# Order of the attention steps in a turn, and of the first slabs of the output projections, in a two-block transformer kernel

## The reference

```python
hn = rmsnorm(x, norm_mix)                      # block 1
x = x + softmax_attention(hn @ w_qkv) @ w_o    # 16 heads of 64, causal
x = x + (silu(conv(gate)) * conv(up)) @ w_down
x = rmsnorm(x, norm_final)
x = x + 0.5 * (1 + ga1) * swiglu(modulate(rmsnorm(x), sh1, sc1))   # block 2
h = modulate(rmsnorm(x), sh2, sc2)
proj = h @ w_in           # q, k, v of 8 stick-breaking and 8 forgetting heads, and f
x = x + (1 + ga2) * concat(stick_breaking(...), forgetting(...)) @ w_o
x = x + 0.5 * (1 + ga3) * swiglu(modulate(rmsnorm(x), sh3, sc3))
```

## Time and profile before

| | |
|---|---|
| median of 3 runs | 852.37 us (851.05 to 853.18) |
| the profiled execution | 851.69 us, of it 849.4 us from the first to the last instruction (span) |
| TensorE matmul, weight load | 810.8 us, 788.7 us busy (95%, 93%) |
| VectorE, ScalarE | 644.5 us, 489.4 us busy (76%, 58%) |
| DMA | 179.44 MB, 211 GB/s in the mean |
| mean granted TensorE clock | 0.995 |

### The profile page before, as it was taken

The page is one execution under the profiler, slowest core; times in us unless marked ns, Lnnn a source line. Parts: engine busy times, 40 slices in busy tenths (PEclk is TensorE's granted clock), DMA queues, the critical chain, the costliest instruction groups (busy, mean ns, idle before and its releaser), DMA issues. The chain is left out here.

```text
span 849.4 us, 16846 instructions
## 1 busy us (share of the span) xinstructions
PE 810.8 (95%) x6824; PEld 788.7 (93%) x6824; DVE 644.5 (76%) x1332; ACT 489.4 (58%) x1015; POOL 21.1 (2%) x53
## 2 busy tenths in 40 slices
PE   5799998999999999999999999899989999999998
PEld 5798887999999999999999999778888999999998
DVE  5687767988898886999888776867657797665551
ACT  6745455767766666755554645655645675555440
POOL 1000000000000000000000002500000000000000
PEclk9999999999999999999999999999999999999999
DMA  9766563865565987599989885545224578665540
GB/s 296 266 220 204 159 202 132 279 195 194 197 220 177 318 279 244 153 317 351 315 290 309 279 262 150 149 130 182 87 76 140 183 255 282 210 197 186 186 150 26
DMA packets 151069, 179.44 MB, mean 211 GB/s; under 512 B 5712, under 2 KB 141136, under 8 KB 150992
## 3 DMA queue, kind: packets, MB, share of 16 engines
q1 hardware_dynamic: 149536, 177.65, 63.7%
q10 hardware_dynamic: 432, 0.68, 0.2%
q0 software_dynamic: 1024, 0.03, 0.1%
HBM read 177.27 MB, written 1.05 MB: 210 GB/s over the span
## 5 line engine op out<-in xcount | busy, mean ns | idle before, releaser
L907 DVE TENSOR_TENSOR wlo<-raw,whi 128x512 fp32r<-128x512 f32 x528 | 343.1, 684 | 71.4 <-ACT whi L669 70.8
L1279 PE MATMUL bank<-A,whi 128*128 128x256 f32 x1280 | 366.5, 286 | 14.6 <-DVE wlo L907 9.0
L669 ACT ACTIVATE whi<-raw 128x512 fp32r<-128x512 f32 x528 | 308.3, 622 | 111.3 <-PE bank L1281 101.5
L1280 PE MATMUL bank<-A,whi 128*128 128x256 f32 x1280 | 358.2, 280 | 0.0
L1281 PE MATMUL bank<-A,wlo 128*128 128x256 f32 x1280 | 358.1, 280 | 0.0
L1279 PEld LDWEIGHTS bank<-A,whi 128*128 128x128 f32 x1280 | 244.6, 191 | 18.5 <-DVE wlo L907 9.6
L1280 PEld LDWEIGHTS bank<-A,whi 128*128 128x128 f32 x1280 | 242.7, 190 | 1.0 <-issue 1.0
L1281 PEld LDWEIGHTS bank<-A,wlo 128*128 128x128 f32 x1280 | 242.3, 189 | 0.0
L1279 PE MATMUL bank<-Hhi,whi 128*128 128x256 f32 x528 | 147.7, 280 | 0.0
L1280 PE MATMUL bank<-Hlo,whi 128*128 128x256 f32 x528 | 147.5, 279 | 0.0
L1281 PE MATMUL bank<-Hhi,wlo 128*128 128x256 f32 x528 | 147.5, 279 | 0.0
(11 more groups left out here) (149 smaller groups left out, 787.8 us busy)
## 6 DMA issues: line engine op xcount, KB each, us to landing
mring<-in_w_mod SPq DMA_DIRECT2D x72, 512.0 KB, 6.2
raw<-in_ffn_w_up SPq DMA_DIRECT2D x22, 1024.0 KB, 5.1
raw<-in_w_gate SPq DMA_DIRECT2D x22, 1024.0 KB, 6.0
raw<-in_w_up SPq DMA_DIRECT2D x22, 1024.0 KB, 5.9
raw<-in_w_down SPq DMA_DIRECT2D x16, 1024.0 KB, 5.4
raw<-in_w_in SPq DMA_DIRECT2D x12, 1024.0 KB, 5.6
raw<-in_moba_w_qkv SPq DMA_DIRECT2D x11, 1024.0 KB, 5.5
raw<-in_ffn_w_down SPq DMA_DIRECT2D x8, 1024.0 KB, 6.0
```

The lines of the kernel that those rows point to most:

```text
L669: act.activation(whi[:, i % SPL, k0:k1, 0:width], raw[:, i % RAW, k0:k1, 0:width], ACT.Copy).then_inc(s_whi, 1)
L907: dve.tensor_tensor(lo, raw[:, i % RAW, k0:k1, 0:width], hi.bitcast(F32), ALU.subtract).then_inc(s_wlo, 1)
L1279: pe.matmul(o, hi, xh, start=kg == 0 and not (j and halved(g)), stop=False)
L1280: pe.matmul(o, hi, xl, start=False, stop=False)
```

## The change

Three parts. (1) In `attend()` the pairs in flight advance first and the new pair enters after them. (2) Pair B enters at A's age 3 in the last blocks too, and in qkv3 the pairs whose slabs lie at columns from 2048 on (the forgetting ones) are unlocked after 3 turns instead of 2. (3) With `O_SPLIT = 3`, o1 and o3 begin with k-tiles 0 to 5 of columns 0, 256 and 512, then k-tiles 6 and 7 of the three, then columns 768 whole; the third group accumulates in bank 4 and waits for the exponentials of head 12 (28) instead of an eviction. One slab more in each phase moves the slab numbers in the conditions by one and by two; the number of `mod` steps in each phase stays.

```diff
--- before.py
+++ after.py
@@ -28,6 +28,7 @@
 VC = {name: 8 * i for i, name in enumerate(VEC)}
 LAST_AGE = 6
 LAG = 1
+O_SPLIT = 3
 RAW = 3
 SPL = 3
 MR = 3
@@ -62,10 +63,10 @@
     def o_slabs(w):
         cut = []
         for lo_k, hi_k in ((0, 6), (6, 8)):
-            for c0 in (0, C):
+            for c0 in range(0, O_SPLIT * C, C):
                 src = w[lo_k * P:hi_k * P, c0:c0 + C].rearrange("(k p) c -> p k c", p=P)
                 cut.append(("o", c0, lo_k, hi_k - lo_k, hi_k == KD, C, src))
-        return cut + slabs_of("o", w, KD, range(0, D, C))[2:]
+        return cut + slabs_of("o", w, KD, range(0, D, C))[O_SPLIT:]
 
     up, down, w_in = a["ffn_w_up"][0], a["ffn_w_down"][0], a["w_in_2"][0]
     allc = range(0, D, C)
@@ -86,9 +87,9 @@
 
 
 MOD_STEPS = {
-    "qkv1": lambda i: int(i > 2) + int(i in (4, 7, 10)), "o1": lambda i: int(i < 17), "up1": lambda i: int(i in (30, 34)),
-    "down1": lambda i: int(i < 51), "up2": lambda i: int(i >= 56) * (1 + int(i % 4 == 0)), "down2": lambda i: int(i < 84),
-    "qkv3": lambda i: int(i in (90, 92, 94, 96)), "o3": lambda i: 0, "up4": lambda i: int(i > 108) * int(i % 2 == 0), "down4": lambda i: 0}
+    "qkv1": lambda i: int(i > 2) + int(i in (4, 7, 10)), "o1": lambda i: int(i < 18), "up1": lambda i: int(i in (31, 35)),
+    "down1": lambda i: int(i < 52), "up2": lambda i: int(i >= 57) * (1 + int(i % 4 == 1)), "down2": lambda i: int(i < 85),
+    "qkv3": lambda i: int(i in (91, 93, 95, 97)), "o3": lambda i: 0, "up4": lambda i: int(i > 110) * int(i % 2 == 0), "down4": lambda i: 0}
 QKV3_TILE = {0: 0, 512: 8, 1024: 16, 1536: 4, 2048: 12, 2560: 20}
 
 
@@ -234,13 +235,12 @@
                 pair[1] += 1
             if flight and flight[0][1] == LAST_AGE:
                 advance(*flight.pop(0))
-            old = list(flight)
-            if waiting and (not flight or flight[-1][1] > (1 if len(self.heads) % 16 > 12 else 2)):
+            for pair in flight:
+                advance(*pair)
+            if waiting and (not flight or flight[-1][1] > 2):
                 enter()
-            for pair in old:
-                advance(*pair)
             turns[0] += 1
-            pend(not any(pair[1] in (3, 4) for pair in old))
+            pend(not any(pair[1] in (3, 4) for pair in flight))
 
         group, o_group, prev = 0, 0, None
         begun, ready = 0, []
@@ -332,7 +332,7 @@
                         st.put("latelo", ph, n - 1)
                     if n == KD - 1:
                         st.put("latelo", ph, n)
-                if scaling and kt % 4 == 3 and i > 56:
+                if scaling and kt % 4 == 3 and i > 57:
                     st.put("xscale", scaling.pop(0))
                 if kt % 2 == 1:
                     done += 1
@@ -356,7 +356,7 @@
                 else:
                     evict(g)
             if tag == "qkv":
-                pending.append(("unlock", ph, c0, turns[0] + 2))
+                pending.append(("unlock", ph, c0, turns[0] + (3 if ph == "qkv3" and c0 >= 2048 else 2)))
             if i + 1 < len(slabs) and slabs[i + 1][0] != ph and ph in NEXT_NORM:
                 norm = NEXT_NORM[ph]
                 if norm == "up1":
@@ -510,6 +510,8 @@
 
         def at(g, i, c0=0, c1=S):
 
+            if groups[g][1] == "o" and groups[g][2] == 2 * C:
+                return banks[S_BANKS[0]][:, i * S + c0:i * S + c1]
             if halved(g):
                 return banks[2 * (g % 2)][:, i * S + c0:i * S + c1]
             return banks[2 * (g % 2) + i][:, c0:c1]
@@ -1266,7 +1268,9 @@
                 kg = k0 + kt
                 need.wait_ge(s_wlo, nth("lo", i, kt // 2))
                 xh, xl, ncol = here(tag, ph, kg, g)
-                if kg == 0:
+                if kg == 0 and tag == "o" and c0 == 2 * C:
+                    need.wait_ge(s_exp, soft[12 if ph == "o1" else 28])
+                elif kg == 0:
                     emptied(need, g - 2)
                 slab = i - plan.first_of[ph]
                 if kt == 0 and (tag == "down" and slab == 0 or ph[:2] == "up" and slab and slab % 4 == 0):
```

## The result

The changed kernel took 854.4 us (median of 20 runs), the kernel before 851.92 us (20 runs beside them). The ratio is 1.0039, with a 95% interval of 1.0024 to 1.0054: slower by 2.5 us, on the edge of what can be told from no change. The forecast was 853.5. The profiled execution took 854.21 us with a span of 852.0, against 851.69 and 849.4.

What follows compares the result with a forecast made beforehand. Product phases were taken as bound by TensorE's matmuls, so only 13.1 us of waits could be won. Terms -2.3 + 2.9 - 2.3 + 0.9 + 2.2 = +1.4 us gave 853.5, range 848.5 to 857.5.

Steps and rivals of the forecast that it cites:

- the sum: Whole kernel: the terms -2.3, +2.9, -2.3, +0.9 and +2.2 add up to +1.4 us.
- Softmax pairs: qkv1, part 1: transposes ahead of new scores gain 0.8 us each in second and third block; qkv1 together -2.3.
- V's transposes: qkv1's softmax blocks: part of the copy wait moves here, 0.4 us; in o3 a new wait of 0.45.
- The new wait for the scaling: qkv1's second and third block: first transposes stand earlier and wait 0.2 us for their scaling.
- First block: qkv1: wait ahead of the transposes grows to about 2.5 us, the 2.09 wait goes; net gain 0.7.
- rival (b): Clock falls behind longer waits in the first block and o3: 855.2 us, second fall 857; chance 0.35 shared with another rival.
- Stick-breaking pairs: Part 1 in qkv3: A's exponential ahead of B's six passes loses 1.1 and 1.75 us, together +2.9.
- line 1209 at 600: Second stick-breaking block: A's product, wanted at 600.6, waits 0.7 us for a VectorE sum.
- A's values: Second stick-breaking block: they wait 0.65 us, the copy of V being done at 609.5 instead of 607.8.
- Forgetting pairs: First forgetting block, part 2: pairs enter one turn later; q and k and copy waits go, -2.3 us.
- The q and k waits: Forgetting scores' waits for normed q and k, 2.2 us, are covered by 12 more matmuls.
- Three groups: o1 and o3, part 3: three evictions in a row make weight remainders wait 2.9 and 5.6 us.

Runs made afterwards that it cites:

- the deferral in o3 alone: Changed kernel with squares, next-product rows and modulation columns of the first three groups put off into the last slab, only in o3: 852.25 us, ratio 1.0003.
- new order alone: Kernel before with only part 1, older pairs advancing before the new pair enters: 852.88 us, ratio 1.0012.
- stick-breaking pairs first: Changed kernel, but stick-breaking pairs enter ahead of the older pairs' steps, as before the change: 850.65 us, ratio 0.9983.
- earlier remainder: Changed kernel, with the third short slab's weight remainder put ahead of the first eviction in o1 and o3: 855.16 us, ratio 1.0048.
- the two kernels of the last group of experiments: Kernel before with parts 1 and 2, stick-breaking pairs entering first: 845.13 us; the same with the condition row's silu two k-tiles earlier: 841.6 us.
- first two parts: Changed kernel without part 3 (`O_SPLIT` at 2): 849.83 us, ratio 0.9973 to the kernel before.
- third part alone: Kernel before with only part 3, six k-tiles of three column groups first: 858.55 us, ratio 1.0073.
- first pair ahead: Changed kernel, but pair B of qkv1's first block enters ahead of the first pair's transposes, as before: 854.38 us, ratio 1.004.
- all three with the deferral: Changed kernel with eviction follow-up work put off: in o1 and o3 (852.59 us), in o3 only (852.25), in both with old stick-breaking order (849.88).
- the kernel with the moved silu: Parts 1 and 2, stick-breaking pairs entering first, and the condition row's silu put two k-tiles earlier: 841.6 us, ratio 0.9882 to the kernel before.
- first two parts with stick-breaking first: Parts 1 and 2 without part 3, stick-breaking pairs entering ahead of older steps: 845.13 us, ratio 0.992 to the kernel before.
- deferral: Changed kernel with squares, next-product rows and modulation columns of the first three groups put off into the last slab, in o1 and o3: 852.59 us, ratio 1.0007.
- deferral with the stick-breaking order: Changed kernel with the eviction follow-up work put off in o1 and o3 and the old order for stick-breaking pairs: 849.88 us, ratio 0.9981.

## Why the prediction was right

The time (853.5 forecast, 854.4 measured) was right to a us and the sum (+1.4 forecast, +2.6 in the spans) to 1.2, and most steps with them. The 1.2 us are the first block's; the errors of the other stretches, up to 0.4 us each, cancel, which is luck.

- *Softmax pairs.* The waits for the first head's copy (L1340 for L859) went, and those of V's transposes came, at 0.23 where 0.4 was walked. The new wait for the scaling in the second and third block was walked at 0.2 and is 0.16. The two blocks gained 1.38, forecast 1.6.
- *First block.* The wait for the scaling was walked at 2.5 and is 2.39. The block was to gain 0.7 and lost 0.52: the clock fell behind this wait. The windows of after (granted clock third from the end) have it:

```profile
36.00:38.00 2.00, 1.29 (x5) 0.96 (x7) 1.84 (x7) 0.69 (x2) 0.00 (x0) 0.69 0.36 72
38.00:40.00 2.00, 2.00 (x13) 1.54 (x12) 0.47 (x2) 1.40 (x2) 0.00 (x0) 0.50 1.06 377
40.00:42.00 2.00, 2.00 (x18) 2.00 (x18) 2.00 (x6) 1.81 (x9) 0.00 (x0) 0.95 0.28 88
```

  By clock, that is 2 x 0.31 + 2 x 0.50 + 2 x 0.05 = 1.7 us, the price of rival (b). In time it was less: the five kernels that fell behind the wait of 2.39 us took 35.0 to 35.4 us to the 193rd product matmul, the three that didn't 34.0 to 34.2, so a fall cost some 1.1 us here. In qkv3 it cost 1.2 and 1.4, read from two pairs of kernels with the same steps there, one of each with the fall. Rival (b) came true here and nowhere else (the fall near 541 us stands in both traces); it is what the sum missed. The fall comes with the transposes that stand directly behind the wait (0.88 us long at 36.71, against 0.55 at the earlier trace rows). By the rule of the Trainium skill, TensorE: Matmul & The Clock Gate, section "Part 4: PE-mode transpose", that order makes a fall likelier; three kernels with the same order and the same 2.39 us kept the clock at 1.00, and no kernel has a wait as long in this block without the transposes behind it, so no run decides it.
- *Stick-breaking pairs.* Forecast 0.7 for line 1209 at 600, measured 0.70 at 599.72; B's second product came from 612.15 to 612.47 although all ahead of it ran 1.66 earlier, so 1.99 in the whole block, forecast 1.75. In the first block 0.67, forecast 1.1. A's values waited 0.45 at 607.96 where 0.65 was walked; the profile names no releaser. The experiment with the old order for these pairs confirms them as the source of 2.7 us in the traces, 3.7 in the medians.
- *Forgetting pairs.* -2.44, forecast -2.3. The q and k waits and the Olo waits went, V's transposes wait 0.42 in o3, forecast 0.45.
- *Three groups.* o3: 1.93, 1.56, 1.54 measured against 2.0, 1.8, 1.75 walked. o1: 0.2, 1.21, 1.06 against 0.2, 1.35, 1.35. So the waits of o1 were 0.4 less, but the stretch took 0.2 more than forecast. Half of the 0.6 us between is that 70 of its matmuls ran at a step longer by 0.0042 us (last section), where before had none; the other half is that behind each of the three waits the second matmul starts 0.22 us after the first, 0.1 more than elsewhere. The prediction had taken the step as fixed and a wait as all that a wait costs; that the two errors of o1 nearly cancel is luck.

What the prediction did not ask is what stood ahead of the first block's scaling: the wait that it took as given hung on one activation and its table load, placed just there.

## What to carry to other kernels

Of a change in three parts, time each part before the whole is judged: here one gained 3 us, one cost 4.6, and one gained in one kind of pair what it lost in the other. When several evictions come in a row, compare their period on the evicting engine (2.7 and 3.1 us here) with the matmul work between them (1.4 us); the difference is the wait, once for each, and taking work out of the head of the chain only moves it. Work that is put off is due somewhere: look at the next consumer (here the norm behind o1, and up4's first slab behind o3, which took back 2.9 of 4.9 us). Behind a long wait look at what stands ahead of the awaited instruction in the lists two engines up: a table load and one activation (2.3 us) moved by two k-tiles gave 3.5 us, some 1.1 of them by a fall of the clock that did not come.

## What was not expected of the hardware

*Two matmul steps at full clock.* Up to qkv3 the changed kernel and the one with the deferral in o3 alone have the same list of instructions. Yet in a stretch of down1 with no waits and a granted clock of 1.00 the first had 91 matmuls in 10 us and the second 87. The window rows, first of after, then of the kernel with the deferral in o3 alone:

```profile
290.00:300.00 10.00, 10.00 (x91) 10.00 (x90) 8.03 (x15) 5.14 (x11) 0.00 (x0) 1.00 0.98 336
```

```profile
290.00:300.00 10.00, 10.00 (x87) 10.00 (x86) 8.48 (x16) 4.60 (x8) 0.00 (x0) 1.00 1.01 349
```

The mean distance of neighbouring starts is 0.1133 us or 0.1175 us, and a slab of 48 matmuls takes 5.44 or 5.65 us. From down1's first matmul, at 266 us in before, to the same matmul near 351 us that makes 85.5 us (before, after, new order alone, stick-breaking pairs first, earlier remainder, and the two kernels of the last group of experiments) or 87.9 (first two parts, third part alone, first pair ahead, and all three with the deferral). The kernel with the first two parts (87.9) and the same with stick-breaking pairs first (85.5) have the same list up to there too. So the step is not fixed by the instructions, and since each kernel has one profiled execution, nothing says that it belongs to the kernel. Later phases choose anew: down2 took 78.0 or 80.3 us, the last phase 59.8 or 62.1. In o1 the longer step goes with the third part: the eight kernels that have it ran 40 to 70 matmuls more at the longer step there, the five without it none. What selects the step stays open: it goes neither with the granted clock nor with the DMA share of these rows, and nothing was tried on it. A change of 2 us in a kernel of 850 has to be read from stretch to stretch for that reason.

Beside it, the fall of the clock at up1's start was longer in four profiles than in the others: from 134 to 150 us the mean granted clock is 0.89 in before and after, 0.79 with the new order alone, the third part alone, the earlier remainder and the kernel with the moved silu. Their first slab of up1 took 7.9 to 8.4 us, the others' 7.0 to 7.3.

*The clock does not fall at a fixed length of wait.* With a wait of 2.39 us at the same place in qkv1's first block, and the same order behind it, it fell in the profiles of five kernels (after, first two parts, stick-breaking first, earlier remainder, first two parts with stick-breaking first) and stayed at 1.00 in three (new order alone, deferral, deferral with the stick-breaking order); in a ninth, the deferral in o3 alone, the wait was 2.53 us and the clock fell. At the wait of 2.9 to 3.0 us in qkv3 it fell in ten and not in three, one of which had 3.01 us. Each is one profiled execution. A fall cost 1.1 to 1.4 us of time where TensorE sets the pace. It cost nothing in o3 with stick-breaking pairs first, where TensorE waits for VectorE anyway: the clock fell to half behind the first eviction wait (at 647 us), and o3 took 34.1 us as in after, which had no fall there.
